# Three attentions of a two-block transformer: key scores in two PSUM banks instead of three, row scores' ring in four instead of three

## What is computed

```python
attn = softmax(s1) - lam * softmax(s2)                      # differential
y_real = window_attn_blocks(q_real, band(k), band(v), ...)  # windowed
sc = jnp.where(kpos[None, :] <= t[:, None], sc, NEG)        # mla: causal
p = jax.nn.softmax(sc, axis=-1)
out = g0 * o_cmp + g1 * o_slc + g2 * o_win                  # nsa: compressed, selected, windowed
```

## Time and profile before

| | us |
|---|---|
| median of 3 runs | 2011.89 |
| lowest, highest | 2010.34, 2013.17 |
| the profiled execution's own time | 2014.6 |
| span of its trace | 2012.5 |
| mean granted clock of TensorE | 0.99 |

### The profile page before, as it was taken

The page is one execution under the profiler, slowest core; times in us unless marked ns, Lnnn a source line. Parts: engine busy times, 40 slices in busy tenths (PEclk is TensorE's granted clock), DMA queues, the critical chain, the costliest instruction groups (busy, mean ns, idle before and its releaser), DMA issues.

```text
span 2012.5 us, 29750 instructions
## 1 busy us (share of the span) xinstructions
PE 1949.4 (97%) x11821; PEld 1067.3 (53%) x11821; DVE 1416.0 (70%) x2420; ACT 948.3 (47%) x1635; POOL 75.3 (4%) x55
## 2 busy tenths in 40 slices
PE   9999999999999999999999999999989999999997
PEld 4444444444444884445444854855444444466476
DVE  6979744538667677777479668778766646966777
ACT  4447723324333344347355335445477843634442
POOL 2000000000000102000000000000000000100000
PEclk9989999999999999999999999999989999999999
DMA  7300223314331333322222341435300031424321
GB/s 244 105 1 1 74 84 107 103 57 143 96 101 51 112 114 125 115 73 64 76 69 81 128 135 53 129 119 145 145 1 1 14 103 34 140 69 153 93 64 43
DMA packets 53930, 179.41 MB, mean 89 GB/s; under 512 B 6176, under 2 KB 11936, under 8 KB 53536
## 3 DMA queue, kind: packets, MB, share of 16 engines
q1 hardware_dynamic: 53792, 177.51, 28.4%
HBM read 174.34 MB, written 2.10 MB: 88 GB/s over the span
## 4 chain that ended last, share of the span: by engine, by line
PE 86%; DVE 10%; issue 2%; ACT 2%; DMA 0%; SPq 0%; DVEq 0%; ACTq 0%
PE pS L1184 12%; PE pS L1185 12%; PE pS L1186 12%; PE pS L1250 4%; PE pS L1251 3%; PE pS L1252 3%; PE pS L1471 3%; PE pO L1506 2%; PE pS L1343 2%; PE pS L1349 2%; PE pS L1344 2%; PE pT L1184 2%; PE pT L1185 2%; PE pT L1186 2%; DVE st_max L2445 2%
## 5 line engine op out<-in xcount | busy, mean ns | idle before, releaser
L2212 DVE SCALAR_TENSOR_TENSOR w_lo<-w_raw,w_hi 128x1024 f16<-128x1024 f32 (+3 forms) x359 | 451.3, 1266 | 59.4 <-ACT w_hi L1749 26.0
L1749 ACT ACTIVATE w_hi<-w_raw 128x1024 f16<-128x1024 f32 (+1 forms) x358 | 372.8, 1062 | 203.8 <-DVE w_raw L2232 83.8
L1184 PE MATMUL pS<-xx,w_hi 128*128 128x512 f16 x952 | 361.3, 380 | 1.4 <-DVE xx L2247 1.4
L1186 PE MATMUL pS<-xx,w_lo 128*128 128x512 f16 x952 | 361.5, 380 | 0.0
L1185 PE MATMUL pS<-xx,w_hi 128*128 128x512 f16 x952 | 361.4, 380 | 0.0
L1250 PE MATMUL pS<-arena,w_hi 128*128 128x256 f16 x645 | 175.8, 273 | 0.0
L1251 PE MATMUL pS<-arena,w_hi 128*128 128x256 f16 x645 | 175.8, 273 | 0.0
L1252 PE MATMUL pS<-arena,w_lo 128*128 128x256 f16 x645 | 175.8, 273 | 0.0
L1186 PEld LDWEIGHTS pS<-xx,w_lo 128*128 128x128 f16 x952 | 93.2, 98 | 112.7 <-issue 0.7
L1184 PEld LDWEIGHTS pS<-xx,w_hi 128*128 128x128 f16 x952 | 93.3, 98 | 109.9 <-DVE xx L2247 2.2
L1185 PEld LDWEIGHTS pS<-xx,w_hi 128*128 128x128 f16 x952 | 93.2, 98 | 107.8 <-issue 1.5
(11 more groups left out here) (450 smaller groups left out, 3812.1 us busy)
## 6 DMA issues: line engine op xcount, KB each, us to landing
w_raw<-in_w SPq DMA_DIRECT2D x298, 512.0 KB, 3.7
w_raw<-in_w SPq DMA_DIRECT2D x12, 704.0 KB, 4.3
X<-in_x SPq DMA_DIRECT2D x8, 264.0 KB, 7.0
arena<-in_c SPq DMA_DIRECT2D x2, 1024.0 KB, 8.6
out_t<-X SPq DMA_DIRECT2D x16, 128.0 KB, 1.7
arena<-in_h SPq DMA_DIRECT2D x4, 256.0 KB, 12.2
arena<-in_h SPq DMA_DIRECT2D x2, 512.0 KB, 10.7
w_raw<-in_w SPq DMA_DIRECT2D x2, 384.0 KB, 3.6
```

The lines of the kernel that those rows point to most:

```text
L1184: pe.matmul(ps, wh, ah, start=f, stop=False)
L1186: mm = pe.matmul(ps, wl, ah, start=False, stop=l)
L1749: act.activation(to_, from_, ACT.Copy, scale=WS).then_inc(hi_split, 1)
L2212: dve.scalar_tensor_tensor(out=lo_[:, a:], in0=from_[:, a:], scalar=WS, in1=hi_[:, a:], op0=ALU.mult, op1=ALU.subtract).then_inc(lo_split, 1)
```

## The change

Key unit u takes bank u % 2 of `pS` and waits for the exp of unit u - 2. `pS` 2 becomes the ring's fourth bank. In mla and nsa row scores and turns take four banks in turn; in mix the row scores rotate over three banks and the turns keep `pT` 1. The value tiles of the lead-ins use banks 0 and 1 in turn. The four query tiles `qn` ahead of mla get banks 3, 2, 1, 0 (before 3, 0, 1, 2), and TensorE waits for one eviction of them more. No engine's instructions change their order or number; lines behind the two new functions stand 8 further down.

```diff
--- before.py
+++ after.py
@@ -72,7 +72,7 @@
 SPARE = ("ks", "qb")
 HOME = {"ck2": 4, "cv2": 5}
 INSIDE = {"va": 0, "vb": NQ, "vm": 0, "vv": 0}
-BANKS = {"ffd0": (5,), "dn0a0": (5, 3), "dn1a0": (5, 3), "dn0b0": (5,), "dn1b0": (5,)}
+BANKS = {"qn": (3, 2, 1, 0), "ffd0": (5,), "dn0a0": (5, 3), "dn1a0": (5, 3), "dn0b0": (5,), "dn1b0": (5,)}
 CLOSED = ("ffd7", "up0a", "up1a")
 UP_A = 16
 
@@ -211,7 +211,7 @@
                 elif s.name in HOME:
                     b = HOME[s.name]
                 elif s.name in INSIDE:
-                    b = (INSIDE[s.name] + j) % 3
+                    b = (INSIDE[s.name] + j) % 2
                 elif s.name == "gt":
                     b = 3
                 else:
@@ -502,9 +502,9 @@
 
         def place(table, key, done, which):
             if name == "mix":
-                b = key % 2 if which == "nat" else 2
+                b = (0, 1, 3)[key % 3] if which == "nat" else 2
             else:
-                b = (own["nat"] + own["turn"]) % 3
+                b = (own["nat"] + own["turn"]) % 4
             own[which] += 1
             table[key] = b
             free[which, key] = last.get(b)
@@ -1020,7 +1020,15 @@
 
         def ring_bank(b):
 
-            return pT[:, b - 1, :] if b else pS[:, 3, :]
+            return (pS[:, 3, :], pT[:, 0, :], pT[:, 1, :], pS[:, 2, :])[b]
+
+        def key_banks(u):
+
+            return 2
+
+        def key_bank(u):
+
+            return pS[:, u % key_banks(u), :]
 
         def y_bank(y):
 
@@ -1453,9 +1461,9 @@
                     pe.wait_ge(evicted, S["vm"].o0 + NQ)
                 if u == RUNS["nsa"].u0:
                     pe.wait_ge(evicted, S["vv"].o0 + NQ)
-                if u >= 3:
-                    pe.wait_ge(key_exped, u - 2)
-                ps = pS[:, u % 3, :]
+                if u >= 2:
+                    pe.wait_ge(key_exped, u - key_banks(u) + 1)
+                ps = key_bank(u)
                 if i == len(t.keys):
                     k0, w = (KC0, NCP) if t.kind.name == "nsa" else (KM0, KM0)
                     for half in range(2):
@@ -1652,7 +1660,7 @@
                 out_T(S["qn"], j, of(cqs))
             pe.wait_ge(zeroed, ZERO_MLA)
             pe.wait_ge(rope_laid, 16 * 8)
-            pe.wait_ge(evicted, S["qn"].o0 + 1)
+            pe.wait_ge(evicted, S["qn"].o0 + 2)
             attention(RUNS["mla"], rest_mla)
             pe.wait_ge(rhs_ready, PL.r["p1"])
             for j in range(KD - 1):
@@ -1895,10 +1903,10 @@
                     a = src[:, t.j % 2, :]
                 else:
                     act.wait_ge(key_scored, u + 1)
-                    a = pS[:, u % 3, :]
+                    a = key_bank(u)
                     if i < len(t.keys):
                         _, c0, _, n = t.keys[i][-1]
-                        a = pS[:, u % 3, 0:c0 + n]
+                        a = key_bank(u)[:, 0:c0 + n]
                 if u >= ring(u):
                     act.wait_ge(unit_av, u - ring(u) + 1)
                 act.activation(exps(u)[:, 0:a.shape[1]], a, ACT.Exp).then_inc(key_exped, 1)
@@ -2471,7 +2479,7 @@
                 dve.wait_ge(key_scored, u + 1)
                 if t.j >= 2:
                     dve.wait_ge(key_exped, u - 2 * 13 + 1)
-                dve.tensor_tensor(src[:, t.j % 2, :], pS[:, u % 3, :], cbias_t[:, t.j // 2, :], ALU.add).then_inc(cmp_biased, 1)
+                dve.tensor_tensor(src[:, t.j % 2, :], key_bank(u), cbias_t[:, t.j // 2, :], ALU.add).then_inc(cmp_biased, 1)
 
             def split_lse(t):
```

## The result

The changed kernel takes 2000.62 us (median of 4 runs, 1998.37 to 2002.82) against 2012.43 of the kernel before (4 runs), a ratio of 0.9938 with a 95% interval of 0.9926 to 0.9950: 12.5 us faster by the ratio. Two later comparisons gave 0.9933 and 0.9934. The forecast was 7.6 us, to 2004.3, with a range of 2000.5 to 2010.5. So the direction was right, and the size too small: 7.6 of 12.5. The profiled execution took 1999.85 us, with a span of 1997.8.

A forecast was written before the change was run, and what follows sets the result against it. TensorE, busy 1949.4 of 2012.5 us, bounds the kernel, with VectorE sharing the bound in the first attention's body. Terms −3.0 + 0.2, + 0.3 − 1.0 + 0.8, + 0.1 − 6.0 + 1.0 sum to −7.6: 2004.3 us, range 2000.5 to 2010.5.

The forecast's parts named there:

- Third attention, body and tail: Third attention: TensorE alone bounds the body, taken −6.0 us; tail keys wait for exps with two banks, taken +1.0.
- the 0.83, 0.3 and 0.07 of the working: Third attention's body: lateness by starts of fifteen row scores, five by 0.83, seven by 0.3, three by 0.07, in all 6.5 us.
- count nothing: Third attention after 1602 us: row-score waits give 0, since the lead would be gone at the next key score.
- TensorE's waits can't all be won, because VectorE takes over: First attention's body: gain bounded by VectorE's waits for scores from 137 us on, 4.0 us; taken −3.0.
- its clock term: Lower granted clock: costs 1.7 us in the first lead-in and 5.8 in the third; change taken 0, ±1.7 per piece.
- the caution about ScalarE: Second attention's body: −1.0 taken of ends 0 and −1.7, since ScalarE is nearly as busy as TensorE there.
- the query banks' order: Before the second attention: new order and one more query eviction wait cost 0, as TensorE waits for VectorE there anyway.
- Two key banks: Key scores wait for the exp two units before: cost 0 in steady parts; tails +0.2, +0.8 and +1.0 us.
- the slack of 0.04: Third attention, key score behind an extra unit: 0.10 us left, less about 0.06 for a release, six times.
- First tail: First attention's tail: four keys with a slack of 0 to 0.2, ends 0 and 0.4 us, taken +0.2.
- rival A: First attention's body: VectorE keeps the pace, body gives 0, waits move to turns; time 2009.9 us; chance 0.22.
- Rival C: First and third lead-ins: lower-clock pieces go with the bank waits, −1.7 and −5.8 us more, 1996.8; chance 0.08.

The follow-up runs named there:

- e1: The kernel before once more, only its tables of banks and waits written differently; ratio to before 0.9998 (0.9989 to 1.0007).
- e2: The changed kernel once more, as it is; median 1999.53 us, ratio to the kernel before 0.9933 (0.9921 to 0.9945).
- e9: The changed kernel again, run beside later variants; median 1998.53 us, ratio to the kernel before 0.9934 (0.9920 to 0.9947).
- e7: The change in the third attention alone, the other two as before; ratio to the kernel before 0.9963 (0.9951 to 0.9975).
- e8: Kernel before with only the lead-ins' value tiles in two banks, old ring kept; ratio to before 1.0003 (0.9995 to 1.0011).
- e3: Two key banks alone: ring and value tiles keep three banks, one bank idle; ratio to the kernel before 1.0006 (0.9998 to 1.0014).
- e11: Changed kernel with four key banks in the tails, taken from the ring; median 1997.48 us, ratio to the kernel before 0.9928.
- e6: The change in the second attention alone, with the new order of the query banks; ratio to the kernel before 0.9994 (0.9986 to 1.0003).

## Why the prediction was right and where it was wrong

| term | forecast | by the stages (e1 to e2, e9 or e7) |
|---|---|---|
| first attention, lead-in and body | −3.0 | −4.0 − 3.6 = −7.6 |
| its tail | +0.2 | +1.2 |
| second: lead-in, body, tail | +0.3 − 1.0 + 0.8 = +0.1 | 0.0 − 1.8 + 1.1 = −0.7 |
| third: lead-in | +0.1 | −0.1 |
| third: body | −6.0 | −8.7 |
| third: tail | +1.0 | +3.3 |
| sum | −7.6 | −12.6 |

Two entries hold a little of the clock. Between stages with equal losses of it, the first attention's lead-in and body give −7.5 (e8 to e2, lead-in 51.79 to 47.97) and the third's lead-in 0.0 (e3 to after), and the sum is −12.3.

- **Third attention, body and tail: mechanism and place right.** 6.9 of the 8.7 us are the waits counted by their starts (6.5 forecast); the steps from before to after at the row scores are the 0.83, 0.3 and 0.07 of the working. The other 1.8 are the last two row scores, behind 1602 us, which were to "count nothing" since "the lead would be gone at the next key score". It was gone: it reappears as the tail's growth. Net, body and tail gave −5.4 against a forecast of −5.0. The two terms were off by 2.7 and 2.3, and 1.8 of each is this lead: won in the one, given back in the other.
- **The step that failed is the first attention's**: "TensorE's waits can't all be won, because VectorE takes over", counted from 137 us on and bounded by VectorE's listed waits for scores, 4.0 (taken −3.0). It measured −7.6 to the last row score and −6.4 with the tail, against −2.8. Two things are wrong in it.
- **First, the bound.** From 137 us of e1, and the same instruction of e2, the traces show 5.8 won to the last row score, 4.6 when the tail has given back 1.2. VectorE did win about what it had waited: its listed waits for scores fell from 4.9 in e1 to 1.4. (The list of before has a fourth row, of 0.4 us, which the 4.0 leaves out.) But to the last row score its busy time fell too, from 80.05 to 78.05, with its idle time from 9.1 to 5.3, and 1.1 of that busy time reappears in the tail (15.28 to 16.38): part of its work fell behind the mark. So its waits for scores don't bound how much earlier TensorE's last row score comes. Over body and tail 0.9 us less of busy time is left, with the same 332 instructions; its cause stays open. This is the row of before that was left out:

```profile
DVE st_max L2445 <- PE pS L1440: 0.4, 1, 0.4
```

- **Second, the term began too late.** Another 1.8 us are won by the first row scores of the lead-in, before 112 us: 1.80 from e8 to e2, which both run at full clock there. The profile of before showed no bank wait at that place, since a piece at the lower clock stood on it. That piece lies before the 132 us at which the working's stretches begin, and is missing from its clock term as well, which has 1.7 us of the 6.8 lost in this lead-in.
- **Second attention:** the body gave 1.8 where the upper end was 1.7; the caution about ScalarE had no ground. The new waits of the lead-in are there, 1.4 us for the value tile and 1.2 behind the query tile, and cost nothing: 25.81 in e1, 25.86 after. The working gave the query banks' order no wait at all; it has one, and later waits for VectorE absorb it.
- **Two key banks:** no cost in the bodies, as forecast (e3). In the tails e3 shows 0.1, 0.8 and 1.5 of cost against 0.2, 0.8 and 1.0. The 0.06 us for a release, on which the slack of 0.04 rests, fits the trace of before: its 26 listed waits of row scores for ScalarE end 0.055 to 0.057 us after the exp.
- **First tail:** of the +1.2, the key banks are 0.1 (e3). The rest is rival A's mechanism at one place. The first turn behind the last row score waits 1.66 us for VectorE's split, and waited 0.5 in e1:

```profile
222.09 0.40 PE L1529 MATMUL pT<-identh,lse_cols 128*128 128x128 f16 x4 [1.66 <-DVE lse_cols L2506]
```

- **Rival C.** The lower-clock pieces did not go: the changed kernel shows them in both lead-ins. Over all executions the clock takes 15.6 us before (66, with e1) and 12.6 after (14), as (1 - clock) times the span, with errors of 0.2 and 0.4. Part of this can't be time: in the first lead-in 3.4 us more of it cost 0.6 (52.54 against 51.93), since waits covered it. The means of the time are 2012.7 and 1999.5, 13.2 apart with an error of 0.4; the stages give 12.3 at equal losses, so 0.9 or so is left for it. That less clock is lost is measured; why was not tried. One place differs: the piece near 140 us stands in all six profiles with the old ring in the first attention, and in four of the seven with the new. That is too few to tell.

By the mechanism of the Trainium skill's page "TensorE: Matmul & The Clock Gate", section "A second HAM failure mode: psum-queue depth-cycling", the bank waits would have had to be the cause of the pieces. The third attention's lead-in shows 6.8 us of them in e2 and in e9, with waits for ring banks of 0.2 us and none left there, so at most a small part is borne out. The Trainium skill's "Perfetto Trace Analysis", section "Matmuls", on rotating groups through banks so that evacuation and matmuls overlap, is borne out for the row scores (waits of 15.5 us fell to 2.1), and for the key scores in the tails alone (2.4 us there, none in the bodies).

## What to carry to other kernels

Give a PSUM bank to the loop whose next matmul stands waiting for it: here four banks served the loop score, maximum, exp, and two were enough for the shorter loop score, exp, as long as both ran. Where the mix of work changes, as at an attention's end, the split should change with it: giving one bank back in the tails was worth another 2.4 us. But a bank handed over while its last user still holds it costs waits, as in e11. Measure a wait by the starts of matmuls, not by the list, and look at a second profile before bounding a stage in which the clock was low: a slow engine shows no waits. And when one engine's idle time is to bound another's gain, say up to which instruction: work can move behind the mark.

## What had not been expected of the hardware

- Stages of 15 to 126 us repeat within 0.1 us from execution to execution when the granted clock is full. What differs between profiles are pieces at the lower clock, 3.4 to 13.7 us long. Inside these attentions they began near 100 and 140, at 1456 to 1473 and, once each, at 224 and 1592 us, present in one execution and absent in the next of the same kernel.
- Such a piece costs little where the engine would have waited anyway. With the old ring the first lead-in took 51.79, 51.93, 52.51, 52.06 and 52.54 us in e8, e1, e3, e6 and before, with 1.7, 3.4, 3.4, 5.1 and 6.8 us of clock lost. In the third attention's tail 1.7 us less clock made it 1.6 longer (28.06 against 26.48).
